# Query and key projections of the even and differential attentions: ten weight tiles as five pairs of seven block products

## The reference, cut to what matters

```python
def even_mixer_2(h, w_in, w_out):
    qkv = (h @ w_in).reshape(B, S, 3, N_HEADS_EVEN, HEAD_DIM).transpose(2, 0, 3, 1, 4)
    q, k, v = rope(qkv[0]), rope(qkv[1]), qkv[2]
...
def diff_mixer(h, w_qkv, lq1, lk1, lq2, lk2, subln, w_out, lambda_init):
    qkv = h @ w_qkv
...
    q, k = rope(q), rope(k)
...
x = x + even_mixer_2(rms_norm_2(x, even_norm[i]), even_w_in[i], even_w_out[i])
```

## Time and profile before

| what | value |
|---|---|
| median of 3 runs | 2256.63 us |
| the profiled execution, its own time | 2258.98 us |
| its span | 2257.2 us |
| PE busy / PE weight loads busy | 2182.3 us (97%) / 1748.5 us (77%) |
| DVE / ACT / POOL busy | 1217.7 (54%) / 1010.3 (45%) / 396.4 us (18%) |
| chain that ended last | PE 89%, ACT 4%, DVE 4%, issue 2%, DMA 1%, POOL 1% |
| mean granted TensorE clock | 0.995 of full speed |

### The profile page before, as it was taken

How to read it: one execution, slowest core, us unless ns; L and a number is a source line. 1 busy time by engine, 2 the same in 40 slices (tenths; PEclk the granted TensorE clock), 3 DMA queues, 4 the chain that set the end, 5 groups by cost and what they waited for, 6 DMA issues and landing times.

```text
span 2257.2 us, 32941 instructions
## 1 busy us (share of the span) xinstructions
PE 2182.3 (97%) x12522; PEld 1748.5 (77%) x12522; DVE 1217.7 (54%) x1862; ACT 1010.3 (45%) x1686; POOL 396.4 (18%) x255
## 2 busy tenths in 40 slices
PE   6999899989999999999999999999999999999998
PEld 3998675678778777877877788888888677888886
DVE  6640566563533107644465566664645855666645
ACT  5431566563355426543275433342432864333323
POOL 1342041001232420030002000024200021000243
PEclk9999999999999999999999999999999999999999
DMA  8122241103321212134301222223243012322221
GB/s 315 57 70 94 86 160 21 45 29 122 122 66 60 88 58 81 62 99 143 116 20 47 94 94 93 93 94 101 95 140 122 20 41 92 97 97 94 94 94 47
DMA packets 59153, 200.92 MB, mean 89 GB/s; under 512 B 8139, under 2 KB 8651, under 8 KB 58764
## 3 DMA queue, kind: packets, MB, share of 16 engines
q1 hardware_dynamic: 59020, 199.08, 26.8%
HBM read 187.19 MB, written 2.10 MB: 84 GB/s over the span
## 4 chain that ended last, share of the span: by engine, by line
PE 89%; ACT 4%; DVE 4%; issue 2%; DMA 1%; POOL 1%; SPq 0%; DVEq 0%; ACTq 0%; POOLq 0%
PE PS L935 7%; PE PS L933 7%; PE PS L934 7%; PE PS L2345 4%; PE PS L3179 4%; PE PS L3177 4%; PE PS L3178 4%; PE PS L2375 3%; PE PS L2006 3%; PE PS L2361 3%; PE PS L1126 2%; PE PS L1128 2%; PE PS L1127 2%; PE PS L1966 2%; PE PS L1268 2%; PE PS L1967 2%
## 5 line engine op out<-in xcount | busy, mean ns | idle before, releaser
L933 PE MATMUL PS<-H_HI,W_SPLIT 128*128 128x512 f32 x672 | 265.5, 395 | 0.0
L935 PE MATMUL PS<-H_HI,W_SPLIT 128*128 128x512 f32 x672 | 264.9, 394 | 0.0
L934 PE MATMUL PS<-H_LO,W_SPLIT 128*128 128x512 f32 x672 | 264.6, 394 | 0.0
L519 POOL TENSOR_TENSOR W_SPLIT<-WT,W_SPLIT 128x1024 fp32r<-128x1024 f32 x43 | 105.2, 2447 | 612.2 <-ACT W_SPLIT L508 495.5
L485 ACT ACTIVATE W_SPLIT<-WT 128x1024 fp32r<-128x1024 f32 x80 | 84.8, 1060 | 267.0 <-PE PS L935 267.0
L3517 DVE TENSOR_TENSOR W_SPLIT<-WT,W_SPLIT 128x1024 fp32r<-128x1024 f32 x80 | 98.0, 1225 | 149.8 <-ACT W_SPLIT L485 149.7
L1334 POOL TENSOR_TENSOR OUT_HALF<-WT,OUT_HALF 128x512 fp32r<-128x512 f32 x48 | 71.3, 1489 | 600.4 <-ACT OUT_HALF L1292 600.4
L3503 DVE TENSOR_TENSOR G_LO<-SB,G_HI 128x512 fp32r<-128x512 f32 x43 | 101.0, 2348 | 108.4 <-ACT G_HI L3323 108.4
L934 PEld LDWEIGHTS PS<-H_LO,W_SPLIT 128*128 128x128 f32 x672 | 126.0, 188 | 30.3 <-issue 0.5
L933 PEld LDWEIGHTS PS<-H_HI,W_SPLIT 128*128 128x128 f32 x672 | 126.2, 188 | 29.9 <-issue 0.5
L935 PEld LDWEIGHTS PS<-H_HI,W_SPLIT 128*128 128x128 f32 x672 | 126.2, 188 | 29.8
(11 more groups left out here) (430 smaller groups left out, 5555.0 us busy)
## 6 DMA issues: line engine op xcount, KB each, us to landing
WT<-weights SPq DMA_DIRECT2D x313, 512.0 KB, 3.6
SB<-SB SPq DMA_DIRECT2D x128, 64.0 KB
SB<-weights SPq DMA_DIRECT2D x13, 512.0 KB, 13.3
XT<-tokens SPq DMA_DIRECT2D x8, 768.0 KB, 6.9
SB<-rpb SPq DMA_DIRECT2D x8, 384.0 KB, 3.9
HT<-rpb SPq DMA_DIRECT2D x8, 384.0 KB, 3.8
out<-HT SPq DMA_DIRECT2D x4, 512.0 KB, 2.7
SB<-late SPq DMA_DIRECT2D x1, 1280.0 KB
```

The lines of the kernel that those rows point to most:

```text
L519: g.tensor_tensor(w[:, 1, :], W[:, (g0 + t) % SLOTS, :], w[:, 0, :].bitcast(F32), ALU.subtract).then_inc(sem("w_lo"), 1)
L933: pe.matmul(PS[:, s, :], hi, H_HI[:, c, :], start=(c == 0), stop=False)
L934: pe.matmul(PS[:, s, :], hi, H_LO[:, c, :], start=False, stop=False)
L935: last = pe.matmul(PS[:, s, :], lo, H_HI[:, c, :], start=False, stop=(c == KC - 1))
```

## The change

Tiles 0 to 5 and the values keep their form. Tiles 6 to 15 become five pairs p = 0 to 4. A pair has four weight blocks of 512 features by 128 outputs, the tokens four blocks of 512 features by 256 tokens (`raw`), and instead of eight block products it makes seven (`Sevens`, named A11, A12, S2, S1, S3, A22, S4 after the weight block or sum of blocks that each takes): each 4 chunks by 3 matmuls of 128x256. Per projection these are 420 matmuls of 256 columns where 240 of 512 stood.

What is added, per projection: ACT multiplies the tokens by their gain into `GX` (`gained`, 8 of 128x512). DVE makes four sums of token blocks in place (`token_sum`), ACT their high parts (`token_hi`), DVE the low parts 0, 1 and 3 and POOL the low part 2 (`token_lo`), each 128x1024. Per pair DVE makes four weight sums (`sums`, 128x512), ACT seven high parts of 128x512 (`hi`), POOL five low parts and DVE two (`lo`, of S2 and S4), ACT copies three partial results (`kept`) and DVE adds four outputs (`out`, one operand in PSUM, 128x256). PE's product S4 waits until outputs 0 and 1 of its pair are written. A product's weight parts lie in one of four half-size buffers in turn.

What is moved: ACT takes tiles 0 to 3 to `QKE` after the Exp of `RC`. The rotations run behind pairs: the tables behind pair 0, tile 0 behind pair 1, tiles 1 and 2 behind pair 2, 3 behind pair 3, 4 and 5 behind pair 4, then two behind each low part of the value tiles 16 to 20. SP's swaps move with them. The product with sin is made in place of the swapped tile.

Core of the diff (`...` marks what is left out):

```diff
+        class Sevens:
+            T0, PAIRS = 6, 5
+            A11, A12, S2, S1, S3, A22, S4 = range(7)
...
+            def by_pool(self, i):
+                return i % 7 not in (self.S2, self.S4)
...
+            def gained(self, act):
+                act.wait_ge(sem("tile_used"), self.g0 + 2)
+                for c in range(KC):
+                    act.activation(self.GX[:, c, :], X[:, c, 0:L], ACT.Identity, bias=NIL, scale=gain_late(self.name, c))\
+                       .then_inc(sem("split_hi"), 1)
+            def token_sum(self, v, n):
+                b11, b12, b21, b22 = (self.raw(k) for k in (0, 2, 3, 1))
+                if n == 0:
+                    v.wait_ge(sem("split_hi"), self.hi0 + 8)
+                else:
+                    v.wait_ge(sem("seven_sum"), self.sum0 + 2 + n)
...
+                v.tensor_tensor(dst, x, y, ALU.subtract).then_inc(sem("seven_sum"), 1)
+            def token_hi(self, act, k):
+                act.wait_ge(sem("seven_sum"), self.sum0 + 2 + (1, 3, 2, 4)[k])
+                act.activation(TOKEN_HI[k], self.raw(k), ACT.Copy).then_inc(sem("split_hi"), 1)
...
+            def sums(self, v, p, k):
+                a, b = self.w(self.T0 + 2 * p), self.w(self.T0 + 2 * p + 1)
+                a11, a12, a21, a22 = a[:, 0:512], a[:, 512:1024], b[:, 0:512], b[:, 512:1024]
+                if k == self.S1:
+                    self.loaded(v, self.T0 + 2 * p + 1)
+                    if p:
+                        v.wait_ge(sem("split_lo"), self.pool_count(7 * (p - 1) + self.S1))
+                    v.tensor_tensor(self.SUM, a21, a22, ALU.add).then_inc(sem("seven_sum"), 1)
+                elif k == self.S3:
+                    self.loaded(v, self.T0 + 2 * p)
+                    v.wait_ge(sem("seven_sum"), self.summed(p, self.S1))
+                    v.tensor_tensor(a21, a11, a21, ALU.subtract).then_inc(sem("seven_sum"), 1)
+                elif k == self.S2:
+                    v.wait_ge(sem("seven_sum"), self.summed(p, self.S3))
+                    v.wait_ge(sem("split_lo"), self.pool_count(7 * p + self.A11))
+                    v.tensor_tensor(a11, self.SUM, a11, ALU.subtract).then_inc(sem("seven_sum"), 1)
...
+            def hi(self, act, i):
+                p, j = self.split(i)
+                if j in (self.A11, self.A12):
+                    self.loaded(act, self.T0 + 2 * p)
+                elif j == self.A22:
+                    self.loaded(act, self.T0 + 2 * p + 1)
+                else:
+                    act.wait_ge(sem("seven_sum"), self.summed(p, j))
...
+                else:
+                    act.wait_ge(sem("seven_done"), self.done0 + i - 4 + 1)
+                act.activation(self.halves_of(i)[0], self.source(i), ACT.Copy).then_inc(sem("split_hi"), 1)
+            def lo(self, eng, i):
+                eng.wait_ge(sem("split_hi"), self.hi_count(i))
+                hi, lo = self.halves_of(i)
+                eng.tensor_tensor(lo, self.source(i), hi.bitcast(F32), ALU.subtract)\
+                   .then_inc(sem("split_lo" if self.by_pool(i) else "split_low"), 1)
...
+            def product(self, pe, p, j):
+                i = 7 * p + j
+                if self.by_pool(i):
+                    pe.wait_ge(sem("split_lo"), self.pool_count(i))
+                else:
+                    pe.wait_ge(sem("split_low"), self.dve_count(i))
+                if p == 0 and j == self.S1:
+                    pe.wait_ge(sem("split_low"), self.low0 + 2)
+                if p == 0 and j == self.A22:
+                    pe.wait_ge(sem("split_low"), self.low0 + 4)
+                if j == self.A11:
+                    if p == 0:
+                        pe.wait_ge(sem("rs_log"), self.i + 1)
+                    else:
+                        pe.wait_ge(sem("qk_raw"), self.raw0 + 4 + 2 * p)
+                if p == 0 and j in (self.S1, self.A22):
+                    pe.wait_ge(sem("qk_raw"), self.raw0 + (5 if j == self.S1 else 6))
+                if j == self.S2:
+                    pe.wait_ge(sem("seven_kept"), self.kept0 + 3 * p + 1)
+                if j == self.S3:
+                    pe.wait_ge(sem("seven_kept"), self.kept0 + 3 * p + 2)
+                if j == self.S4:
+                    pe.wait_ge(sem("seven_out"), self.out0 + 3 * p + 2)
...
+                for c in range(4):
+                    thi, tlo = self.tokens(j, c)
+                    hi, lo = whi[:, c * 128:c * 128 + 128], wlo[:, c * 128:c * 128 + 128]
+                    one = pe.matmul(dst, hi, thi, start=first and c == 0, stop=False, skip_group_check=True)
+                    if j == self.S4 and c == 0:
+                        one.then_inc(sem("tile_used"), 2)
+                    pe.matmul(dst, hi, tlo, start=False, stop=False, skip_group_check=True)
+                    last = pe.matmul(dst, lo, thi, start=False, stop=final and c == 3, skip_group_check=True)
+                last.then_inc(sem("seven_done"), 1)
+            def kept(self, act, p, k):
+                act.wait_ge(sem("seven_done"), self.done0 + 7 * p + (self.A11, self.S2, self.S3)[k] + 1)
...
+            def act(self, act):
+                for p in range(self.PAIRS):
+                    i = 7 * p
+                    self.kept(act, p, 0)
+                    self.hi(act, i + 4)
+                    self.hi(act, i + 5)
+                    self.kept(act, p, 1)
+                    self.hi(act, i + 6)
+                    if p + 1 < self.PAIRS:
+                        self.hi(act, i + 7)
+                    self.kept(act, p, 2)
+                    if p + 1 < self.PAIRS:
+                        for j in range(8, 11):
+                            self.hi(act, i + j)
+            def pool(self, g):
+                for i in range(7 * self.PAIRS):
+                    if i == self.S1:
+                        self.token_lo(g, 2)
+                    if self.by_pool(i):
+                        self.lo(g, i)
...
+            def dve(self, v, roped):
+                self.sums(v, 0, self.S2)
+                self.sums(v, 0, self.S4)
+                self.lo(v, self.S2)
+                self.token_lo(v, 3)
+                for p in range(self.PAIRS):
+                    more = p + 1 < self.PAIRS
+                    self.out(v, p, 0)
+                    if more:
+                        self.sums(v, p + 1, self.S1)
+                        self.sums(v, p + 1, self.S3)
+                    self.lo(v, 7 * p + self.S4)
+                    if more:
+                        self.sums(v, p + 1, self.S2)
+                    self.out(v, p, 1)
+                    self.out(v, p, 2)
+                    if more:
+                        self.sums(v, p + 1, self.S4)
+                        self.lo(v, 7 * p + 7 + self.S2)
+                    self.out(v, p, 3)
+                    roped(p)
...
+                swaps = {13: (0, 1, 2, 3), 15: (4,), 17: (5, 6), 19: (7,), 21: (8, 9), 23: (10, 11), 24: (12, 13, 14, 15)}
+                for t in range(8, 25):
                     one(self.g0 + t)
-                    if t == 10:
-                        self.swap(sp, 0)
-                        self.swap(sp, 1)
-                    if t >= 10:
...
+                    if t == 6:
+                        self.sevens.pe(pe)
+                    if 6 <= t < 16:
+                        continue
...
+                        if t in (16, 17):
+                            act.wait_ge(sem("seven_done"), self.sevens.done0 + 7 * self.sevens.PAIRS - 17 + t)
...
+                        self.sevens.gained(act)
...
                     k = t - 2
-                    if 0 <= k < 16:
-                        act.wait_ge(sem("tile_used"), self.g0 + k + 1)
-                        act.activation(QKE[:, k, :], PS[:, k % 6, :], ACT.Copy).then_inc(sem("qk_raw"), 1)
+                    if t == 5:
+                        for r in range(4):
+                            self.take(act, r)
...
+            def seven_act(self, act):
+                self.sevens.token_hi(act, 0)
+                self.sevens.hi(act, 0)
+                self.sevens.hi(act, 1)
+                self.sevens.token_hi(act, 1)
+                self.sevens.token_hi(act, 2)
+                self.take(act, 4)
+                self.sevens.token_hi(act, 3)
+                self.sevens.hi(act, 2)
+                self.sevens.hi(act, 3)
+                self.take(act, 5)
+                self.sevens.act(act)
...
-                for t in range(4, 24):
-                    self.low(v, t)
-                    if t == 5:
+                self.low(v, 4)
+                self.sevens.sums(v, 0, Sevens.S1)
+                self.sevens.sums(v, 0, Sevens.S3)
+                self.sevens.token_sum(v, 0)
+                self.low(v, 5)
+                self.sevens.token_sum(v, 1)
+                self.sevens.token_lo(v, 0)
+                self.sevens.token_sum(v, 2)
+                self.sevens.token_sum(v, 3)
+                self.sevens.token_lo(v, 1)
+                def roped(p):
```

(26 more changed lines are left out.)

139 lines of the change are left out of this document (118 added, 21 removed).

## The result

The changed kernel takes 2313.47 us (median of 4 runs, 2312.46 to 2314.31) against 2256.56 for the kernel before (4 runs): a ratio of 1.0249, 95% interval 1.0237 to 1.0262. It is **slower by 56.9 us**; 2303.6 was forecast, 47.0 more than before, within a range of 2262 to 2326. The profiled execution took 2312.46 us by its own time, 53.5 us more than that of before.

A forecast was written before the change was run, and what follows sets the result against it. PE, busy 97% of the span, was taken to bound the kernel. Terms summed to +25.3 us in e2_in and +21.7 in df_in, together +47.0, giving 2303.6 us at the level of the runs; range 2262 to 2326.

The forecast's parts named there:

- b): Tile 5's high part stands behind eight gained copies on ACT, so PE begins it later: +4.4 us e2_in, +3.4 df_in.
- c): Filling pair 0, tile 5 to S2: POOL and DVE work by turns makes S2 late, +8.3 us e2_in, +5.7 df_in.
- d): S4 of pair 0 waits for outputs behind POOL and DVE work: 9.6 us from S2's start instead of 5.6, +4.0.
- e): S4 of pairs 1 to 3 can start at 9.4 + 0.6 n us against 8.4: +2.2, +2.8, +4.6; last pair 0.
- f): Tile 16's low part on DVE stands behind output 3 of the last pair and two rotations: +5.6 us.
- a): Per projection, 420 matmuls of 256 columns at 0.1167 us replace 240 at 0.2318: gain 6.6 us, 13.2 over both.
- Rival 1: POOL and DVE run beside each other and only queue order counts: +14.7 us, 2271; chance 0.12.
- rival 3: PE's clock falls after each of some twelve waits: +16 us, up to 20, giving 2320 to 2324; chance 0.10.
- Rival 2: The waits of b) to f) are all covered, only the products' gain stays: 2243.4 us; chance 0.06.
- Rival 4: Unhidden weight loads on PE cost 0.13 us more per matmul: +109, 2413; chance 0.01; half, at 0.128 a matmul, +9.5.
- What was costed at nothing: ACT's high parts and copies, takes of 16 and 17, SP's swaps, weights, later rotations: 0; late swaps up to 6 us.

The follow-up runs named there:

- the best version: Changed kernel with low parts on DVE, gained copies and tile 16's low part earlier, pair 0 reordered, rotations spread, table products ahead of pair 0; 2249.28 us.
- the last experiment: the best version with tile 16's low part behind output 3 and rotations 4 and 5 again; 2263.10 us, 13.8 over it.

## Why the prediction was right, and where it was off

The table sets the terms against the changed kernel's trace. A measured term is the distance between two starts on PE less what the same products take at full clock, so it holds the waits and what the slow clock adds inside that stretch. Full clock is 1.40 us for a product and 5.56 for a tile.

| term | forecast e2_in, df_in | measured |
|---|---|---|
| b) tile 5 begins later | +4.4, +3.4 | +4.4, +3.1 |
| c) tile 5 to S2 of pair 0 | +8.3, +5.7 | +7.7, +5.1 |
| d) S2 to S4 of pair 0 | +4.0, +4.0 | +3.2, +3.5 |
| e) A11 to S4, pair 1 | +2.2, +2.2 | +2.3, +1.4 |
| e) pair 2 | +2.8, +2.8 | +2.7, +2.9 |
| e) pair 3 | +4.6, +4.6 | +4.6, +4.5 |
| e) pair 4 | 0, 0 | +1.4, +1.3 |
| f) S4 of pair 4 to tile 16 | +5.6, +5.6 | +5.8, +5.8 |
| the four S4 of pairs 0 to 3 themselves | 0, 0 | +1.8, +2.5 |
| tile 16 itself | 0, 0 | +1.4, +3.0 |
| sum with a) at -6.6 | +25.3, +21.7 | +28.7, +26.5 |

The two projections lost 55.2 us in the trace; the span grew by 53.4, so the rest of the program gave back under 2, of which 1.4 lie in the wait for the first weights (16.4 us before, 15.0 after). The medians are 56.9 apart and not 53.5, because the profiled execution of the kernel before lies 2.4 us over its median and that of the changed kernel 1.0 under.

**a) Products.** The pace was that of the earlier trace rows inside a product, 0.12 us. In the best version the 35 products of e2_in take 51.0 us from the first start to tile 16's, with 0.9 of short waits, mostly ahead of S4; a product takes about 1.43 us where 12 x 0.1167 = 1.40 was used. So the gain is 5.5 us without those waits and 4.6 with them, where 6.6 stood. The three steps of 0.35 us that the price was read from could not tell 0.1167 from 0.119, and 420 times the difference is 1 us. Twice 4.6 is 9.2; 13.2 us had been there to gain, and 8.0 were gained by the medians.

**b) and f)** were read off the order of a queue and the durations of its instructions, and came out within 0.3 us each. The early copies and the early low part took them away.

**c), d), e)** rested on the exclusion of POOL and DVE, with the bound that all of it could be absent. The low parts on DVE removed 27 us, POOL's return to the best version cost 15.5. The step holds. Rival 1, that nothing excludes and only order counts, is settled against, and the earlier trace rows were read rightly. In c) and d) the measured stretches are 0.5 to 0.8 us shorter than worked out; which item of those sums was too long was not taken apart. Two readings inside them need care. In e2_in the low part of S2 is done at 1046.83 and the copy that S2 waited for at 1047.39, behind two high parts and a take on ACT: the last 0.6 us of c) there are ACT's, which the sum had down as covered. And the +3.2 of d) in e2_in is 0.2 of waiting and 3.0 of slow products behind the wait at S2; only df_in, with 3.2 us of waiting behind products at full pace, shows d) by itself.

**The clock** is the term that the sum left out. The prediction had it as rival 3 and as an either-or: the whole sum, or the sum and 16 to 20 us. It is neither. What the clock takes behind a wait shortens the next one where that is set by DVE and POOL: tile 5 of e2_in ran 2.5 us longer, and S2, which DVE and POOL made ready at their own pace, was waited for 5.1 us and not 7.7. Only where no later wait swallows it does the loss stay: behind the S4 waits, in pair 4, in tile 16. The lines of the table that were forecast as 0 hold it, 1.4 + 1.8 + 1.4 in e2_in and 1.3 + 2.5 + 3.0 in df_in, 11.4 us with some of the pace of a). All other lines together came out 1.2 and 2.0 us under the sum. 11.4 - 3.2 is the 8.2 us by which the trace's 55.2 exceed 47.0. The mechanism named in rival 3 is right; its size was too large, for not every wait brings the clock down and a later wait takes up what some cost, and it belonged in the sum, for the waits behind which nothing waits again. So 47.0 is near 55.2 because the other terms were good to 3.2 us in all, and the shortfall is this one term, with some of the pace of a).

**Rival 2** (everything hides) fails as the change stands and comes near for the same products with the low parts on DVE and another order: 2249.3 us, where it had 2243.4. Its argument, that ev_in runs with PE never idle, was sound about the scheme. What differed was the load: per pair 9.8 us of operations that exclude each other in 9.8 us of products, which the earlier trace rows with 14.65 us a pair could not warn of without the division that the rival made. Rival 4, a weight load that shows, is out with the pace of a); what it calls half, 0.128 us a matmul, is a tenth of the further 0.13 (half would have been some +55 us), which changes nothing at its chance of 0.01. What was costed at nothing, ACT, SP's swaps and the weights, held in all nine changed kernels but for ACT's 0.6 us in c): no wait of PE in the pairs is for a swap or a weight tile, and the one for ACT is the copy ahead of S2 of pair 0, late with all that stands before it.

## What to carry to other kernels

Two engines that exclude each other are one engine: here POOL, and DVE where both its inputs lie in SBUF. Count these operations in one sum; a low part that costs 0.60 us on DVE and 1.24 on POOL is better on DVE, even where DVE is the busier. When products shrink, read what stands in each queue ahead of the first part of each product; here the move to DVE was worth 27.2 us by itself, a low part ahead 11.9, copies ahead 8.3, and all edits together, with the new order of pair 0, the rotations and the tables, which were not measured singly, 64; the scheme itself is worth 8. And a wait of PE of some 5 us is to be priced with 1.3 to 2.5 us of lower clock behind it (the last experiment), unless a later wait absorbs that.
